# The attention of a hybrid layer: the last two value tiles of a step, a fold and the third turned group take other places

## The reference

```python
def one_block(qi):
    s = jnp.einsum('bkgqd,bksd->bkgqs', qi, kt).astype(jnp.float32) * scale
    p = jax.nn.softmax(s, axis=-1).astype(vt.dtype)
    return jnp.einsum('bkgqs,bksd->bkgqd', p, vt)
```

## Time and profile before

| | before |
|---|---|
| median of 3 runs | 2780.42 us (2778.55 to 2780.79) |
| the profiled execution | 2782.8 us, span 2781.0 us |
| PE busy | 2698.0 us, 97% of the span |
| DVE, ACT, POOL busy | 1482.7, 627.9, 541.7 us |
| mean granted TensorE clock | 0.994 |

### The profile page before, as it was taken

One profiled execution on the slowest core, in us unless ns is written; L12 is line 12 of the kernel. 1 busy time (PEld: TensorE's weight loads), 2 busy tenths in 40 slices (PEclk: granted clock), 3 DMA queues, 4 the chain that ended last, 5 costly groups with the idle time before them and its releaser, 6 DMA issues.

```text
span 2781.0 us, 35088 instructions
## 1 busy us (share of the span) xinstructions
PE 2698.0 (97%) x14088; PEld 2202.9 (79%) x14088; DVE 1482.7 (53%) x2349; ACT 627.9 (23%) x1152; POOL 541.7 (19%) x468
## 2 busy tenths in 40 slices
PE   8999999999999999999999989999999999999998
PEld 3888888888888867877777777777778888888887
DVE  6645444344443474167655688867444444444444
ACT  4200000000000044243345688851110000000002
POOL 0065456465420000005420032220000000000001
PEclk9999999999999999999999999999999999999999
DMA  8112112222211122111233100025201111111112
GB/s 294 38 65 65 61 57 73 87 87 91 91 47 37 40 85 66 50 57 62 84 116 107 63 1 1 16 84 161 82 24 53 45 45 53 45 46 52 45 45 76
DMA packets 198289, 187.67 MB, mean 67 GB/s; under 512 B 7645, under 2 KB 149770, under 8 KB 198026
## 3 DMA queue, kind: packets, MB, share of 16 engines
q1 hardware_dynamic: 190160, 171.83, 19.4%
q10 hardware_dynamic: 7994, 13.97, 1.3%
HBM read 161.39 MB, written 24.38 MB: 67 GB/s over the span
## 4 chain that ended last, share of the span: by engine, by line
PE 86%; DVE 6%; ACT 4%; issue 2%; DMA 1%; ACTq 0%; POOL 0%; DVEq 0%; SPq 0%
PE psum L221 26%; PE psum L222 25%; PE psum L223 25%; DVE ptl L1995 2%; PE psum L1876 1%; ACT pth L1945 1%; PE psum L314 1%; ACT prob L1928 1%; PE psum L1500 1%; PE psum L1894 1%; PE psum L1893 1%; PE psum L408 1%; DVE wl L198 1%; PE psum L570 0%; DMA raw<-in_w_out_dram 0%
## 5 line engine op out<-in xcount | busy, mean ns | idle before, releaser
L221 PE MATMUL psum<-nh,wh 128*128 128x512 f32 (+2 forms) x1688 | 627.7, 372 | 1.4 <-DVE wl L198 1.4
L222 PE MATMUL psum<-nl,wh 128*128 128x512 f32 (+2 forms) x1688 | 613.8, 364 | 0.0
L223 PE MATMUL psum<-nh,wl 128*128 128x512 f32 (+2 forms) x1688 | 613.3, 363 | 0.0
L814 ACT ACTIVATE silu_a<-psum 128x512 f32<-128x512 f32 (+1 forms) x110 | 61.2, 556 | 1494.2 <-PE psum L223 1494.2
L196 DVE CAST wh<-raw 128x1024 fp32r<-128x1024 f32 (+1 forms) x173 | 122.4, 708 | 492.9 <-PE psum L223 492.8
L221 PEld LDWEIGHTS psum<-nh,wh 128*128 128x128 f32 (+1 forms) x1688 | 317.3, 188 | 65.9 <-issue 7.1
L222 PEld LDWEIGHTS psum<-nl,wh 128*128 128x128 f32 (+1 forms) x1688 | 317.2, 188 | 52.7 <-issue 4.1
L223 PEld LDWEIGHTS psum<-nh,wl 128*128 128x128 f32 (+1 forms) x1688 | 316.8, 188 | 52.3
L846 DVE SCALAR_TENSOR_TENSOR h<-psum,gates,h 128x512 f32<-128x512 f32 (+1 forms) x400 | 270.9, 695 | 155.9 <-PE psum L223 153.7
L221 PE MATMUL psum<-hidh,wh 128*128 128x512 f32 (+1 forms) x880 | 331.3, 376 | 11.1 <-DVE hidl L830 7.6
L222 PE MATMUL psum<-hidl,wh 128*128 128x512 f32 (+1 forms) x880 | 326.7, 371 | 0.0
(11 more groups left out here) (258 smaller groups left out, 3769.1 us busy)
## 6 DMA issues: line engine op xcount, KB each, us to landing
raw<-in_w_ffn_up_dram SPq DMA_DIRECT2D x88, 512.0 KB, 3.9
mod_part<-in_w_mod_dram SPq DMA_DIRECT2D x96, 256.0 KB, 4.2
raw<-in_w_ffn_down_dram SPq DMA_DIRECT2D x44, 512.0 KB, 3.7
raw<-in_w_in_dram SPq DMA_DIRECT2D x34, 512.0 KB, 3.9
mod_raw<-in_w_mod_dram SPq DMA_DIRECT2D x12, 1024.0 KB, 13.9
gates_saved<-staged ACTq DMA_DIRECT2D x40, 256.0 KB, 2.0
merge_gate<-gates_saved SPq DMA_DIRECT2D x8, 1024.0 KB, 5.2
x_rows<-in_x_dram SPq DMA_DIRECT2D x8, 512.0 KB, 8.1
```

Source lines behind the costliest of these rows:

```text
L221: pe.matmul(o, hi_w, hi_x, start=first, stop=False)
L222: pe.matmul(o, hi_w, lo_x, start=False, stop=False)
L223: return pe.matmul(o, lo_w, hi_x, start=False, stop=last)
L814: nc.scalar.activation(silu_a[:, c, 0:w], ps[c][:, 0:w], ACT.Silu).then_inc(self.a_free, 1)
```

## The change

Four things change, all in the attention steps.

1. Group 2 of a block is copied by ACT from PSUM into a new SBUF tile `third` (two slots of 128x256), and GpSimd makes the high and the low part from it. DVE no longer makes this low part. The next group in the same bank waits for ACT's copy (`p_hi`) in place of the low part.
2. PE multiplies three value tiles where it multiplied five, and the other two behind the latent scores at the end of the step. In odd steps the tile that ends the pair, and with it `pv_done`, is among these two. They wait for GpSimd's part as well (`third_lo`).
3. ACT runs `fold` behind the high copies of groups 0 and 1, where it ran ahead of them.
4. GpSimd's queue gets two instructions for each block, ahead of the pair's three.

```diff
@@ -1009,6 +1009,7 @@
     probs = [at("prob0", 92, [TOK]), at("prob1", 97, [TOK]), at("prob2", 160, [TOK])]
     att_t = at("att_t", 136, [2, 2, 256])
     att_rb = at("att_rb", 205, [2, 256])
+    third = at("third", 102, [2, 256])
     prob_first = at("prob_first", 128, [TOK])
     mtot, nmax = at("mtot", 182, [64, 2]), at("nmax", 182.5, [64])
     rs = at("rs", 207, [64, 2])
@@ -1816,6 +1817,7 @@
         sem(n) for n in ("s_lat", "s_ctx", "mx_done", "nm_done", "exp_lat", "exp_ctx", "rt_done", "ri_done"))
     rb_done, a_norm = sem("rb_done"), sem("a_norm")
     t_done, p_hi, p_lo, pv_done = (sem(n) for n in ("t_done", "p_hi", "p_lo", "pv_done"))
+    third_hi, third_lo = sem("third_hi"), sem("third_lo")
     ot_done, os_done, a_hi, a_lo = (sem(n) for n in ("ot_done", "os_done", "a_hi", "a_lo"))
     Q_BLOCKS = SEQ // P
     N_STEP = HEADS * Q_BLOCKS
@@ -1869,9 +1871,10 @@
             pe.wait_ge(exp_lat, i + 1)
             for r in groups:
                 a, b = TGROUPS[r]
-                n = TG * i + r
-                if n >= 2:
-                    pe.wait_ge(p_lo, n - 1)
+                if r == 1 and i >= 1:
+                    pe.wait_ge(p_hi, TG * i)
+                elif r == 2 or i >= 1:
+                    pe.wait_ge(p_lo, 2 * i + (1 if r == 2 else 0))
                 for kt in range(a, b):
                     mm = pe.transpose(turned_of(i, r)[:, (kt - a) * P:(kt - a + 1) * P],
                                       prob(i)[:, kt * P:(kt + 1) * P], ident)
@@ -1879,7 +1882,9 @@
 
         def values(v, tiles):
             kv = 2 * v // Q_BLOCKS // (HEADS // KV_HEADS)
-            pe.wait_ge(p_lo, 2 * TG * (v + 1))
+            pe.wait_ge(p_lo, 4 * (v + 1))
+            if K_TILES - 1 in tiles:
+                pe.wait_ge(third_lo, 2 * (v + 1))
             if v >= 1:
                 pe.wait_ge(os_done, v)
             o = ps[7][:, 0:256]
@@ -1909,11 +1914,14 @@
                 score(i + 1, True)
             if i >= 4:
 
-                values((i - 4) // 2, range(5, K_TILES) if i % 2 else range(0, 5))
+                tiles = range(5, K_TILES) if i % 2 else range(0, 5)
+                values((i - 4) // 2, tiles[0:3])
             if 2 <= i <= N_STEP:
                 turn(i - 1, (0, 1))
             if i + 2 < N_STEP:
                 score(i + 2, False)
+            if i >= 4:
+                values((i - 4) // 2, tiles[3:5])
             if i in EARLY_MERGE:
                 merge_early_pe(pe, merge_p0, EARLY_MERGE.index(i))
 
@@ -1942,6 +1950,11 @@
             for r in groups:
                 a, b = TGROUPS[r]
                 act.wait_ge(t_done, TG * i + r + 1)
+                if r == 2:
+                    if i >= 2:
+                        act.wait_ge(third_lo, i - 1)
+                    nc.scalar.activation(third[:, i % 2, :], turned_of(i, 2), ACT.Copy).then_inc(p_hi, 1)
+                    continue
                 nc.scalar.activation(pth[:, v % 2, a:b, (i % 2) * P:(i % 2 + 1) * P],
                                      turned_of(i, r).rearrange("p (k q) -> p k q", q=P), ACT.Copy).then_inc(p_hi, 1)
 
@@ -1965,10 +1978,10 @@
                 high(i - 2, (2,))
             if 1 <= i < N_STEP:
                 exp_latent(act, i)
+            if 1 <= i <= N_STEP:
+                high(i - 1, (0, 1))
             if i >= 5 and i % 2 == 1:
                 fold((i - 5) // 2)
-            if 1 <= i <= N_STEP:
-                high(i - 1, (0, 1))
 
     def maxima(dve, i):
         dve.wait_ge(s_lat, i + 1)
@@ -1991,6 +2004,8 @@
             v = i // 2
             a, b = TGROUPS[r]
             q = slice((i % 2) * P, (i % 2 + 1) * P)
+            if r == 2:
+                return
             dve.wait_ge(p_hi, TG * i + r + 1)
             nc.vector.tensor_tensor(ptl[:, v % 2, a:b, q], turned_of(i, r).rearrange("p (k q) -> p k q", q=P),
                                     pth[:, v % 2, a:b, q].bitcast(F32), ALU.subtract).then_inc(p_lo, 1)
@@ -2034,7 +2049,26 @@
     MERGE_SPLITS = (27, 28)
 
     def att_pool(pool):
+        a, b = TGROUPS[2]
+
+        def third_group(i):
+            v, q = i // 2, slice((i % 2) * P, (i % 2 + 1) * P)
+            whole = third[:, i % 2, :].rearrange("p (k q) -> p k q", q=P)
+            pool.wait_ge(p_hi, TG * (i + 1))
+            if v >= 2:
+                pool.wait_ge(pv_done, v - 1)
+            nc.gpsimd.tensor_copy(pth[:, v % 2, a:b, q], whole).then_inc(third_hi, 1)
+            pool.wait_ge(third_hi, i + 1)
+            nc.gpsimd.tensor_tensor(ptl[:, v % 2, a:b, q], whole, pth[:, v % 2, a:b, q].bitcast(F32), ALU.subtract)\
+                .then_inc(third_lo, 1)
+
+        third_group(0)
+        third_group(1)
         for v in range(N_PAIR):
+            for i in (2 * v + 2, 2 * v + 3):
+                if i < N_STEP:
+                    third_group(i)
+            pool.wait_ge(third_lo, min(2 * v + 4, N_STEP))
             hd, qb = divmod(v, Q_BLOCKS // 2)
             rows = slice(HD * (hd % 2), HD * (hd % 2) + HD)
             q = slice(qb * 256, (qb + 1) * 256)
@@ -2047,11 +2081,10 @@
             pool.wait_ge(a_hi, v + 1)
             nc.gpsimd.tensor_tensor(al[rows, hd // 2, q], att_t[rows, 1, v % 2, :],
                                     ah[rows, hd // 2, q].bitcast(F32), ALU.subtract).then_inc(a_lo, 1)
+            pool.wait_ge(a_lo, v + 1)
             if v in GLA_SPLITS:
-                pool.wait_ge(a_lo, v + 1)
                 gla_split_pool(pool, GLA_SPLITS.index(v))
             if v in MERGE_SPLITS:
-                pool.wait_ge(a_lo, v + 1)
                 early_split_pool(pool, merge_p0, MERGE_SPLITS.index(v))
 
 
```

## The result

The changed kernel takes 2832.67 us (median of 4 runs, 2829.34 to 2835.27), the kernel before 2780.61 us in the same comparison. The ratio is 1.0188, with a 95% interval of 1.0170 to 1.0205. It is slower, as forecast, but by 52 us where 9.7 were forecast, and far outside the range.

The account below looks back on a forecast made before the run. No engine was full; a chain between PE, ACT and DVE set the pace. Pairs going from 8.34 to 8.69 us put step 63 9.7 us later, so the median 2780.42 became 2790.1 us, range 2784 to 2799.

Parts of the forecast that it names:

- What bounds the kernel: Attention windows: no engine is full; a chain between PE, ACT and DVE sets the pace, 8.34 us a pair on average.
- The chain of distances: Start-to-start times along one pair of attention steps in the kernel before: 4.16 + 4.07 = 8.23 us.
- Third group at nothing: Group 2's low part moved from DVE to GpSimd: off the chain, so no time gained or lost.
- the walk: One pair of attention steps of the changed kernel followed through these distances: 8.69 us, against 8.34 before.
- Tiles and fold: Odd step: transposes 0.48 us earlier, high copy at 1.91 us instead of 2.69; the later `pv_done` delays the fold.
- The stall before the context scores: PE waits there for ACT's context exponential in every second step, about 1.4 us; waits of about 1.2 us were to show.
- Rival 3: PE's clock falls to its low level once in each head: 20 us on top, 2810 us; chance 3%.
- The sum: Steps 4 to 63: 28 pairs of 8.69 us plus the end steps; step 63 starts 9.7 us later, median 2790.1 us.
- the walk's own stall: Loss over the attention stage from PE's wait before the context scores: 9.7 us in all.
- DVE and the shared access: DVE's `rtot` and GpSimd instructions may exclude each other; some tenths of a us, within DVE's spare time, sum unchanged.
- rival 2: DVE becomes the bound as GpSimd's 0.73 us instructions stand before `rtot`: 9 us more, 2799 us; chance 12%.
- Rival 1: Fold starts right behind the two high copies, so doesn't hold the scores: pair 7.84 us, 2766 us; chance 8%.

Follow-up runs that it names:

- three other orders: Changed kernel with the finer wait, 2786.0 us; with odd steps' value tiles back ahead of the transposes, 2779.08 us; that plus fold ahead of the high copies, 2766.78 us.
- the finer wait: Changed kernel, but high copies of groups 0 and 1 wait for a new semaphore given with value tile 7 in place of `pv_done`: 2786.0 us, ratio 1.0024.

## Why the prediction was right or wrong

**What bounds the kernel.** Right. The chain of distances gave each step of before, and the same distances gave the pairs of three other orders: 8.69 against 8.62, 8.32 against 8.28 to 8.44, 7.85 against 7.82 to 7.94.

**Third group at nothing.** Right as far as it was run: 2777.2 us with it alone, and the walk that took it at nothing gave the pair with the finer wait. Beside the even steps' tiles it is worth about 9 us, since DVE's queue then ends late for the low part of group 0.

**Tiles and fold: the step that failed.** The prediction put it so: "ACT is ready at 0.79 ... + 1.00 ... + 0.09 ... = 1.88. So PE decides: 1.91". ACT's queue was free then, but its next instruction, the high copy, also waits for `pv_done`. The code (L1941 of the kernel before) and ScalarE's rows in the order before the result both show this wait. I followed `pv_done` to the fold only. Before the change it cost nothing, since the tile was multiplied ahead of the transposes. Behind the latent scores the last tile starts 3.39 after the step's start, and the copy 3.70. The finer wait shows what it costs: 46.7 us with the clock it brought down, and 46.7 - 14.0 = 32.7 without.

**The stall before the context scores.** Right in mechanism: with the finer wait it is 1.2 us in each pair, as written. In the changed kernel it shrank to 0.66, since PE was held up ahead of it.

**The clock.** Rival 3 had 3% and 20 us. It came on top of the missed wait: 14 us. In the changed kernel PE stands idle twice in a pair, 1.50 and up to 0.66; with one stand of about 1.2 per pair the clock stayed at 1.00.

**The sum.** 52 us is, as far as the runs divide it: 5.4 for the walk's own stall (2786.0 - 2780.6; 6.3 against the 2779.7 of that run's own comparison; the walk said 9.7), 32.7 for the missed wait, 14.0 for the clock. The walk's own term was 3 to 4 us too large. In the run with the finer wait the pair measured 0.07 less than walked, 2 us over the stage (253.7 from step 4 to step 63, where the walk had 255.6), and step 4 came 1.2 us sooner behind the first scores than before. The rest is within the spread of the runs. So "slower" was forecast for a stall that gives about a tenth of the loss; the direction came out by that and by the wait that was left out.

**DVE and the shared access.** `rtot` lasted at most 0.41 us in the changed kernel, 0.16 in the middle, so rival 2 did not come. Rival 1 needed the last tile before the fold's turn. The fold did stand right behind the two high copies, 0.97 to 1.11 behind the first, but only because these copies had waited for the last tile themselves, so nothing was gained. A fold that starts before 1.5 was the sign that the prediction had named for a walk wrong in its main step.

## What to carry to other kernels

When an instruction that signals is moved, list every wait on that semaphore, also those that cost nothing now, and walk each one; a wait that guards a slot of a double buffer is as real as one for data. A wait on the last piece of a group can often be a wait on the piece that is really overwritten: here one such edit was worth 47 us. A walk from start to start of the rows of one period, with queue order and waits, gave other orders to within 4 us when no wait was left out, and missed by 29 and 43 us the two times one was.

## What the runs showed of the hardware that was not expected

In the changed kernel the lower TensorE clock came back in 9 of the 29 pairs with no idle stretch of PE longer than 1.5 us, and each time the plain step took 6.02 to 6.20 us where it takes 4.45 to 4.62. Six repeated matmuls in each longer idle stretch, whose results change nothing, took 14 us off the whole. With an idle stretch of 2.3 us in each pair it came back in 10 pairs, so the length of the idle stretch alone does not say how often. Summed over a pair, the two kernels in which it came back are near each other: PE stood idle for 2.0 to 2.2 and for 2.3 to 2.4 us. In the kernel before and in all other runs it was at most 1.4 us, and there the clock stayed at 1.00 through the running steps. What brings it down in some pairs and not in others stays open.
